# Eight of sixteen u and z weight tiles moved behind the backward sweep's chunks, and the high half of each weight tile as a converting copy written out per tile

## What is computed

```python
def ssm_project(h, w_in, ...):
    z, xbc, dt_raw, u = jnp.split(h @ w_in, IN_SPLITS, axis=-1)   # z: gate, u: pooling input, 1024 columns each
    ...
def bidir_ssd(xs, dt, a_log, bm, cm, h0_f, h0_b):
    y_f, s_f = ssd_chunked(xs, dt[:, :, 0], a[0], bm, cm, h0_f)                 # forward
    y_b, s_b = ssd_chunked(rev(xs), rev(dt[:, :, 1]), a[1], rev(bm), rev(cm), h0_b)  # backward
    return y_f + rev(y_b), s_f, s_b
def mixer_out(y_scan, xs, z, u, ...):
    y = (y_scan + d_skip * xs) * silu(z) ...
    pm = pool_mixer(u, ...)
    return concat([rmsnorm(y), pm]) @ w_out
```

## Time and profile before

| | us |
|---|---|
| median of 3 runs | 3521.98 |
| lowest, highest | 3518.48, 3525.23 |
| the profiled execution | 3518.24 |
| its span in the trace | 3516.4 |
| PE busy | 2964.3 |
| DVE busy | 1556.9 |
| Pool busy | 973.8 |

### The profile page before, as it was taken

One profiled execution on the slowest core, in us unless ns is written; L12 is line 12 of the kernel. 1 busy time (PEld: TensorE's weight loads), 2 busy tenths in 40 slices (PEclk: granted clock), 3 DMA queues, 4 the chain that ended last, 5 costly groups with the idle time before them and its releaser, 6 DMA issues. The chain is left out here.

```text
span 3516.4 us, 35911 instructions
## 1 busy us (share of the span) xinstructions
PE 2964.3 (84%) x13838; PEld 2448.1 (70%) x13838; DVE 1556.9 (44%) x1676; ACT 574.4 (16%) x680; POOL 973.8 (28%) x417
## 2 busy tenths in 40 slices
PE   4877867987999999996896798957578799999996
PEld 3766755776888888875773477755467677778875
DVE  6365463235222222245756656646744522222225
ACT  2212213121100010012221122221111100000001
POOL 0220221312334343340221022212222244444341
PEclk9978978978999999995998799978787899999997
DMA  3111113101212122121001112231110011111111
GB/s 117 42 56 46 46 51 133 40 30 54 72 60 66 65 62 69 60 66 68 31 24 36 48 72 83 79 131 64 61 72 30 26 46 48 48 47 42 48 46 56
DMA packets 60726, 205.49 MB, mean 58 GB/s; under 512 B 10160, under 2 KB 13488, under 8 KB 60400
## 3 DMA queue, kind: packets, MB, share of 16 engines
q1 hardware_dynamic: 39072, 140.16, 11.9%
q10 hardware_dynamic: 21584, 64.40, 5.3%
HBM read 173.99 MB, written 29.36 MB: 58 GB/s over the span
## 5 line engine op out<-in xcount | busy, mean ns | idle before, releaser
L188 POOL TENSOR_TENSOR w_hi<-w_raw,zeros 128x1024 fp32r<-128x1024 f32 x206 | 397.2, 1928 | 2470.2 <-PE ps L202 2435.7
L198 PE MATMUL ps<-a_hi,w_hi 128*128 128x512 f32 x2176 | 695.1, 401 | 107.8 <-PEq L2147 21.6
L200 PE MATMUL ps<-a_lo,w_hi 128*128 128x512 f32 x2176 | 683.9, 395 | 0.0
L202 PE MATMUL ps<-a_hi,w_lo 128*128 128x512 f32 x2176 | 683.3, 395 | 0.0
L191 POOL TENSOR_TENSOR w_lo<-w_raw,w_hi 128x1024 fp32r<-128x1024 f32 x206 | 576.8, 2800 | 16.2
L198 PEld LDWEIGHTS ps<-a_hi,w_hi 128*128 128x128 f32 x2176 | 413.8, 193 | 193.3 <-issue 110.9
L200 PEld LDWEIGHTS ps<-a_lo,w_hi 128*128 128x128 f32 x2176 | 417.4, 192 | 89.5
L202 PEld LDWEIGHTS ps<-a_hi,w_lo 128*128 128x128 f32 x2176 | 416.2, 191 | 88.7
L198 PE MATMUL ps<-g_hi_b,w_hi 128*128 128x512 f32 x1120 | 355.9, 399 | 103.3 <-DVE g_lo_b L2098 56.6
L200 PE MATMUL ps<-g_lo_b,w_hi 128*128 128x512 f32 x1120 | 352.8, 397 | 0.0
L202 PE MATMUL ps<-g_hi_b,w_lo 128*128 128x512 f32 x1120 | 351.8, 396 | 0.0
(11 more groups left out here) (379 smaller groups left out, 2731.0 us busy)
## 6 DMA issues: line engine op xcount, KB each, us to landing
w_raw<-in_wstream SPq DMA_DIRECT2D x206, 512.0 KB, 3.5
ada_w<-in_ada_w ACTq DMA_DIRECT2D x50, 512.0 KB, 3.5
y_by_token<-y ACTq DMA_DIRECT2D x16, 512.0 KB, 3.2
tmp_b<-mixer_out SPq DMA_DIRECT2D x8, 512.0 KB, 3.4
x_res_b<-in_xT SPq DMA_DIRECT2D x1, 4096.0 KB, 14.4
x_block<-x_res_b SPq DMA_DIRECT2D x8, 512.0 KB, 2.6
y<-y_by_token ACTq DMA_DIRECT2D x8, 512.0 KB, 3.3
u_rows<-ada_w ACTq DMA_DIRECT2D x8, 512.0 KB, 2.7
```

What stands on the lines that cost most here:

```text
L188: pool.tensor_tensor(k.w_hi[:, s, :], k.w_raw[:, s, :], k.zeros[:, 0:1].broadcast_to([P, KT * P]), ALU.add).then_inc(k.w_high, 1)
L198: pe.matmul(o, w_hi, a_hi[:, c], start=first, stop=False)
L200: pe.matmul(o, w_hi, a_lo[:, c], start=False, stop=False)
L202: ins = pe.matmul(o, w_lo, a_hi[:, c], start=False, stop=last)
```

## The change

The eight backward chunks are written out on PE, ACT and DVE, and behind each of them PE does one u or z tile (tiles 0 to 7 of the sixteen). ACT issues the y store first, then copies the next chunk's `CT` and `Bt`, then evacuates and stores the tile. The forward sweep becomes four turns of two chunks; each chunk has one of the remaining eight tiles, whose first half of the token columns stands between B0 and F1 and whose second half between B1 and ST. ACT evacuates it behind the exponentials.

In `stream_split` the high half becomes a `tensor_copy` to the fp32r tile in place of the addition, the loop is written out per tile, and every tile from the third on waits for n - 1 tiles done, in the first stage as well.

```diff
 def stream_split(pool, k, first, last):
-    with pool.Fori(0, (last - first) // 2) as j:
-        for s in range(2):
-            n = first + 2 * j + s
-            pool.wait_ge(k.w_loaded[s], (j + first // 2 + 1) * 16)
-            if first:
-                pool.wait_ge(k.tile_done, n - 1)
-            else:
-                pool.wait_ge(k.tile_done, 2 * j)
-            pool.tensor_tensor(k.w_hi[:, s, :], k.w_raw[:, s, :], k.zeros[:, 0:1].broadcast_to([P, KT * P]),
-                               ALU.add).then_inc(k.w_high, 1)
+    for n in range(first, last):
+        s = n % 2
+        pool.wait_ge(k.w_loaded[s], (n // 2 + 1) * 16)
+        if n >= 2:
+            pool.wait_ge(k.tile_done, n - 1)
+        pool.tensor_copy(k.w_hi[:, s, :], k.w_raw[:, s, :]).then_inc(k.w_high, 1)
...
+        FWD_TILES = XBC_END + NC
...
-            with pe.Fori(0, NC) as i:
+            for i in range(NC):
...
                     ins = add_state(X[1], Bt[:, g, :], g)
                 ins.then_inc(s["x_done"], 1)
+                gemm(pe, k, XBC_END + i, i % 2, XBC_END // 2 + i // 2, v.a_hi, v.a_lo)
...
-                gemm(pe, k, XBC_END + 2 * i, 0, XBC_END // 2 + i, v.a_hi, v.a_lo)
+                pe.wait_ge(k.w_split, FWD_TILES + i + 1)
+                pe.wait_ge(k.pair_free[q], FWD_TILES // 2 + jj)
+                first, second = both_halves(k, q)
+                tile_products(pe, k, q, v.a_hi, v.a_lo, [first])
                 decays(F1, 2, TRI_LE)
                 decays(B1, 3, TRI_GE)
-                gemm(pe, k, XBC_END + 2 * i + 1, 1, XBC_END // 2 + i, v.a_hi, v.a_lo)
+                tile_products(pe, k, q, v.a_hi, v.a_lo, [second]).then_inc(k.tile_done, 1)
                 job(ST)
...
+            for i in range(NC):
                 c = NC - 1 - i
...
                 act.wait_ge(s["y_ready"], i + 1)
+                act.dma_start(d.y_tok[c, :, :], y[:, :]).then_inc(s["y_out"], 16)
+                if i + 1 < NC:
+                    act.wait_ge(s["x_done"], back + BWD_JOBS * (i + 1))
+                    backward_rows(c - 1)
+                staged(XBC_END + i, i % 2, i // 2, XBC_END // 2 + i // 2)
...
                 exps(F0, 0)
                 act.wait_ge(s["off_added"], i + 1)
                 exps(B0, 1)
-                staged(0, ACT.Copy, d.u_scr)
                 exps(F1, 2)
                 act.wait_ge(s["w_ready"], 2 * i + 1)
                 exps(B1, 1)
-                staged(1, ACT.Silu, d.z_scr)
+                staged(FWD_TILES + i, q, NC // 2 + jj, FWD_TILES // 2 + jj)
```

More of the change, by code:

```diff
@@ L178, in stream_split @@
 def stream_split(pool, k, first, last):
-    with pool.Fori(0, (last - first) // 2) as j:
-        for s in range(2):
-            n = first + 2 * j + s
-            pool.wait_ge(k.w_loaded[s], (j + first // 2 + 1) * 16)
-            if first:
-                pool.wait_ge(k.tile_done, n - 1)
-            else:
-                pool.wait_ge(k.tile_done, 2 * j)
-            pool.tensor_tensor(k.w_hi[:, s, :], k.w_raw[:, s, :], k.zeros[:, 0:1].broadcast_to([P, KT * P]),
-                               ALU.add).then_inc(k.w_high, 1)
-            pool.wait_ge(k.w_high, n + 1)
-            pool.tensor_tensor(k.w_lo[:, s, :], k.w_raw[:, s, :], k.w_hi[:, s, :].bitcast(F32),
-                               ALU.subtract).then_inc(k.w_split, 1)
+    for n in range(first, last):
[4 more added lines that the diff above has]
+        pool.tensor_copy(k.w_hi[:, s, :], k.w_raw[:, s, :]).then_inc(k.w_high, 1)
+        pool.wait_ge(k.w_high, n + 1)
+        pool.tensor_tensor(k.w_lo[:, s, :], k.w_raw[:, s, :], k.w_hi[:, s, :].bitcast(F32),
+                           ALU.subtract).then_inc(k.w_split, 1)
 def products(pe, w_hi, w_lo, a_hi, a_lo, outs, first, last):
@@ L1671, in _, with forward @@
             ctx_states(CC + NC, (NC, NC + 1))
-            with pe.Fori(0, NC) as i:
+            def forward(jj, q):
+                i = 2 * jj + q
                 def job(j):
@@ L1711, in _ @@
                 ins.then_inc(s["x_done"], 1)
+            with pe.Fori(0, NC // 2) as jj:
+                forward(jj, 0)
+                forward(jj, 1)
         @block.scalar
@@ L1719, in b_rows, with staged, backward_rows, forward @@
                 return chunk(v.tok, c, slice(0, VAL)).rearrange("p (g n) -> p g n", g=NGRP)
-            with act.Fori(0, NC) as i:
+            def staged(tile, q, pair_no, freed_before):
+                func, out = ((ACT.Copy, d.u_scr), (ACT.Silu, d.z_scr))[q]
+                act.wait_ge(k.tile_done, tile + 1)
+                act.wait_ge(s["u_out"], 16 * (tile - XBC_END))
+                act.activation(stage[:, :], pair[q], func).then_inc(k.pair_free[q], 1)
+                act.wait_ge(k.pair_free[q], freed_before + 1)
+                act.dma_start(out[bass.ds(pair_no, 1), :, :].rearrange("a p n -> p (a n)"), stage[:, :])\
+                   .then_inc(s["u_out"], 16)
+            def backward_rows(c):
+                current(CT, v.bc[:, NGRP:2 * NGRP, c * P:(c + 1) * P])
+                current(Bt, b_rows(c))
+            act.wait_ge(s["x_done"], back)
+            backward_rows(NC - 1)
+            for i in range(NC):
                 c = NC - 1 - i
-                act.wait_ge(s["x_done"], back + BWD_JOBS * i)
-                current(CT, v.bc[:, NGRP:2 * NGRP, bass.ds(c * P, P)])
-                current(Bt, b_rows(c))
                 act.wait_ge(s["y_ready"], i + 1)
-                act.dma_start(d.y_tok[bass.ds(c, 1), :, :].rearrange("a p n -> p (a n)"), y[:, :]).then_inc(s["y_out"], 16)
-            with act.Fori(0, NC) as i:
+                act.dma_start(d.y_tok[c, :, :], y[:, :]).then_inc(s["y_out"], 16)
[3 more added lines that the diff above has]
+                staged(XBC_END + i, i % 2, i // 2, XBC_END // 2 + i // 2)
+            def forward(jj, q):
+                i = 2 * jj + q
                 act.wait_ge(s["x_done"], fwd + J * i)
@@ L1738, in exps @@
                     act.activation(E[:, to, :], Xf[j % 2], ACT.Exp).then_inc(x_free[j % 2], 1)
[L1740 to L1747, removed]
                 exps(F0, 0)
@@ L1755, in _ @@
                 exps(B1, 1)
-                staged(1, ACT.Silu, d.z_scr)
+                staged(FWD_TILES + i, q, NC // 2 + jj, FWD_TILES // 2 + jj)
                 act.wait_ge(s["y_ready"], NC + i + 1)
                 act.dma_start(d.y_tok[bass.ds(i, 1), :, :].rearrange("a p n -> p (a n)"), y[:, :]).then_inc(s["y_out"], 16)
+            with act.Fori(0, NC // 2) as jj:
+                forward(jj, 0)
+                forward(jj, 1)
             act.wait_ge(s["y_out"], 16 * 2 * NC)
@@ L1787, in _ @@
             from_ctx(1, (ALL_C - 1, ALL_C - 2), 0)
-            with dve.Fori(0, NC) as i:
-                ch.enter(i, 3)
+            for i in range(NC):
                 c = NC - 1 - i
@@ L1803, in _, with forward @@
                 dve.wait_ge(x_free[1], back // 2 + i + 1)
-                ch.leave(NC)
             from_ctx(0, (NC, NC + 1), fwd_ctx)
-            with dve.Fori(0, NC) as i:
-                ch.enter(i, 10)
+            def forward(jj, q):
+                i = 2 * jj + q
                 def done(j):
@@ L1863, in _ @@
                 dve.sem_inc(s["y_ready"], 1)
-                ch.leave(NC)
+            with dve.Fori(0, NC // 2) as jj:
+                ch.enter(jj, 20)
+                forward(jj, 0)
+                forward(jj, 1)
+                ch.leave(NC // 2)
 def phase6(nc, k, d, w):
```

## The result

The changed kernel takes 3440.7 us (median of 4 runs, 3439.0 to 3441.4) beside 3523.6 us for the kernel before (4 runs, 3518.5 to 3525.2): ratio 0.9769, 95% interval 0.9756 to 0.9781, so 2.3% faster. The profiled executions are 77.6 us apart, 3518.2 and 3440.6.

What follows compares the result with a forecast made beforehand. TensorE (PE), busy 84% of the span, was taken as the bound. Gains 20 (phase 5) + 5.9 + 4.4 + 12.6 + 3.2 = 46.1 us off 3518.2 give 3472.1, plus 3.7 for the median: 3476 us, range 3442 to 3508.

Steps and rivals of the forecast that it cites:

- Backward sweep, +40: Phase 5's backward sweep: a tile behind each chunk makes chunks PE-bound at 14.4 us, costing 40 us.
- Forward sweep, -60: Phase 5's forward sweep: one tile fewer per chunk cuts the period from 42.1 to 34.6 us, saving 60 us.
- the collision: Forward chunk's end: Pool's split and DVE's weights and state operations exclude one another, adding 2.7 us per chunk.
- S: Forward chunk: start of the second half tile, from which the listed DVE and Pool step times count.
- Last MLP, -5.9: Last MLP: the shorter w_hi lets PE restart 0.74 us sooner in eight steps, gaining 5.9 us.
- rival 4: Collisions fall into slack and PE's clock holds behind MLP gaps: 22 us in phase 5, up to 10 in MLP; 3444; chance 0.13.
- First MLP, -4.4: First MLP: PE's wait for g_lo, 4.4 us in all, goes entirely with the shorter w_hi.
- First stage, -15.8: Stretch up to the first MLP: 12.6 us of w_lo waits and 3.2 us of blocked table work gained.
- The w_lo term: First stage: PE's four waits for Pool's late w_lo vanish with the new n - 1 waits, gaining 12.6 us.
- the table work's: First stage: DVE's table work between heads is blocked less by Pool's splits, net gain 3.2 us.
- Rival 1: MLPs: with a copy under about 0.9 us, w_lo starts before DVE's tmp_b, +7.7 instead of -10.3; 3494 us; chance 0.2.
- Rivals 2, 3 and 5: Forward sweep gives back gain, 3504, chance 0.12; slow Pool copy, 3559, 0.07; copy costs what the addition did, 3493, 0.08.

Runs made afterwards that it cites:

- the hold: The changed kernel with Pool's split of a tile in the forward sweep waiting until y's last addition of the chunk: 3427.8 us, ratio 0.9738.
- the copy alone: The kernel before with w_hi as a copy and the loop written out, but with the old waits: 3483.2 us, ratio 0.9901.
- the waits alone: The kernel before with the written-out split waiting for n - 1 tiles also in the first stage, w_hi still an addition: 3502.4 us, ratio 0.9954.
- The half copy: The changed kernel with only the first 512 of 1024 columns of w_hi copied from the third tile on: 3460.1 us, ratio 0.9834.

## Why the prediction was right in direction and short in size

The forecast was 3476 us, 46 us faster; measured are 3440.7 us, 35 below it and 1.3 below the range's low end of 3442. Faster was given 0.89. Of the 35 us, 11.6 arose up to the first MLP, 9.8 in the forward sweep, 8.9 in the last MLP and 2.4 in the first; 3.8 are the step from the profiled execution to the median.

- **Backward sweep, +40:** measured +41.0. The chunk is PE-bound at 14.36 us, everything else lies under the tile. Right.
- **Forward sweep, -60:** measured -69.8. The mechanism was right, down to which DVE operation waits; the size of the collision was off. Its steps came a little sooner each than listed (with S at 2079.77: w_hi until 7.6 for 7.9, w_lo until 10.8 for 11.25, y's addition until 14.3 for 14.8), and the hold showed 1.8 us (14.5 / 8) for the 2.7 taken. 33.5 - 31.1 - 1.8 leaves 0.6 for the 0.8 put down to the clock; no run isolates that rest, but PE's busy time per chunk, less the tile taken out, rose by 0.4 (225.1 us for 310.0 - 8 x 11.0). 1.1 us too much, times 8, is 8.8 of the 9.8.
- **The copy's duration:** 1.1 taken, 1.04 measured. Right.
- **Last MLP, -5.9:** measured -14.8. The gap shrank by 5.7 us in all, as forecast. The step that failed is the sentence "I add nothing for a clock that may fall less": the half-rate stretches behind six of the eight gaps were 9.6 us, and all of them went. The rows for it were there: the gap's neighbours run at half rate in the kernel before. I had put it into rival 4 at up to 10 us, and it belonged in the sum as its own term.
- **First MLP, -4.4:** measured -6.8, and again -6.8 with the copy alone. PE's wait for g_lo gives 4.4, as forecast; of the other 2.4 us 0.8 are a shorter wait for acc_b (9.5 to 8.7) and 1.6 PE's busy time (816.8 to 815.2).
- **First stage, -15.8:** measured -27.4 up to the first MLP's start. PE's waits in the stretch fell by 20.9 us (209.1 to 188.2 in sum), its busy time by 6.4 (616.5 to 610.1). The w_lo term (12.6) was right; the table work's was 6.1 (42.1 to 36.0) for 3.2. Other waits gave 2.2. What I left out is the clock again, at the largest price: behind each of the four waits for w_lo PE ran four to six pairs of products at half rate, 7.1 us in all, and with the waits alone its busy time fell by 7.0. The copy alone gave 16.1 us and the waits alone 22.1, together only 27.4. PE's waits for the tables show part of that overlap: they fell by 10.0 us with the copy, by 3.1 with the waits and by 6.1 with both.
- **Signs named in advance:** the products 14.4 us apart, w_hi at 1.1 and the wait for g_lo near 1.5 came as said; the forward period was to be 34 to 35 and is 33.5; the first CB was to come near 2008 and came at 1995.4, as the stages ahead of it had gained more.
- **Rival 1** (Pool first at the port) did not come about in the changed kernel: margin 0.16 us. The half copy brought it about and came out 19 us above the changed kernel; 18 had been foreseen, but without the clock and without the forward sweep's 4.6 us, so the number is partly luck. **Rival 4** came in half: the clock's part whole, the forward part by 9 of 22 us. **Rivals 2, 3 and 5** fell with the copy's 1.04 us and the period of 33.5.

Open: the 3.1 us of PE's busy time that the copy alone adds in the first stage, and why the first stage's parts overlap by 13.0 us (40.4 and 27.4).

## What to carry to other kernels

Fill idle time of the bounding engine from a stage that has none: eight tiles cost 41 us behind a serial chain and saved 70 where they stood. Where Pool and DVE both read SBUF, ask of each pair of their instructions who starts first: here 0.43 us less work on Pool cost about 20 us, and two waits that hold Pool back, which add no work, gained about 20. Ask it anew in each stage: the copy made twice lengthened the MLPs and shortened the forward sweep. When an edit shortens a gap in front of PE, read PE's rate behind that gap in the old trace (here behind four waits in the first stage and six in the last MLP), and put the half-rate stretch into the sum if it is there.

## What was new about the hardware

GpSimd's copy with conversion to fp32r, 128 x 1024, takes 1.04 us, against 1.89 for an addition of a broadcast zero. In the last MLP a gap of 2.3 us between two busy stretches of PE was followed by four to five pairs of products at half rate in six of eight cases, one of 1.6 us in none of eight. Of a Pool and a DVE instruction that both read SBUF the one issued first ran unhindered: 0.16 us ahead of w_lo a DVE multiplication took 1.22 us, 0.26 us behind it 3.23.
